# Low parts on GpSimd, a gate in three passes, shorter means, and residual work moved in a two-block transformer kernel

## The reference, cut to what matters

```python
h = x @ w_in + b_in                       # 1024 -> conv_a, conv_g, q, k, v, r, f_lr, gate_a, gate_b
u = a * sigmoid(g)
u = depthwise_conv(u, 31 taps) + conv_b
u = silu(layer_norm(u, ln_g, ln_b))       # mean and variance over the 1024 channels
y_conv = u @ w_co + b_co
y_gla = gla_branch(q, k, v, r, f_lr, ...) @ w_o
merged = sigmoid(gate_a) * y_conv + sigmoid(gate_b) * y_gla
x = layer_norm(alpha * x + merged @ w_out + b_out, ln1_g, ln1_b)
x = layer_norm(alpha * x + hier_moe(x), ln2_g, ln2_b)   # 64 experts, 8 groups, top 2 of one group
# then the second block (four branches, a feed-forward layer)
```

## Time and profile before

| | us |
|---|---|
| median of 3 runs | 1696.02 (1695.73 to 1697.38) |
| the profiled execution, whole | 1695.62 |
| its span in the trace | 1693.5 |
| PE, DVE, ACT, POOL busy in the span | 1361.7, 674.6, 472.0, 58.8 |

### The profile page before, as it was taken

One profiled execution on the slowest core, in us unless ns is written; L12 is line 12 of the kernel. 1 busy time (PEld: TensorE's weight loads), 2 busy tenths in 40 slices (PEclk: granted clock), 3 DMA queues, 4 the chain that ended last, 5 costly groups with the idle time before them and its releaser, 6 DMA issues.

```text
span 1693.5 us, 21308 instructions
## 1 busy us (share of the span) xinstructions
PE 1361.7 (80%) x8592; PEld 883.3 (52%) x8592; DVE 674.6 (40%) x1109; ACT 472.0 (28%) x682; POOL 58.8 (3%) x27
## 2 busy tenths in 40 slices
PE   8999999876666756666676666566799999999998
PEld 7889988522122212221221222122399999778887
DVE  4788979311001101110110011011267888655874
ACT  4464233401001001000010010010264864456653
POOL 0000000670000000000000000000000000000000
PEclk9999999889788879887887888888899999999999
DMA  8433555799999999999999999999944325475440
GB/s 345 152 144 150 213 206 247 307 432 429 431 431 431 433 431 432 432 432 431 430 433 433 432 432 431 432 430 432 421 188 150 131 73 196 174 254 176 180 174 25
DMA packets 50441, 530.79 MB, mean 313 GB/s; under 512 B 4276, under 2 KB 5556, under 8 KB 33862
## 3 DMA queue, kind: packets, MB, share of 16 engines
q1 hardware_dynamic: 50374, 529.86, 75.6%
HBM read 528.80 MB, written 1.05 MB: 313 GB/s over the span
## 4 chain that ended last, share of the span: by engine, by line
PE 53%; DMA 36%; DVE 6%; ACT 3%; issue 1%; DVEq 0%; SPq 0%; ACTq 0%
DMA shared<-in_w 36%; PE psum L1429 6%; PE psum L454 6%; PE psum L456 6%; PE psum L455 6%; PE psum L367 5%; PE psum L1450 4%; PE psum L2216 4%; PE psum L1456 3%; PE psum L1402 3%; PE psum L2217 2%; PE psum L2053 1%; DVE ring_parts L590 1%; PE psum L611 1%; PE psum L2187 1%
## 5 line engine op out<-in xcount | busy, mean ns | idle before, releaser
L1429 PE MATMUL psum<-ring,arena 128*32 128x512 f32 x992 | 142.7, 727 | 85.5 <-DMA ring<-in_w 85.4
L1429 PE MATMUL psum<-shared,arena 128*32 128x512 f32 x1040 | 147.8, 712 | 63.4 <-DMA shared<-in_w 63.3
L1659 DVE TENSOR_TENSOR shared<-shared,psum 128x512 f32<-128x512 f32 x16 | 11.0, 689 | 457.4 <-PE psum L1429 457.4
L1450 PE MATMUL psum<-shared 128*32 128x512 f32 x512 | 90.5, 843 | 67.0 <-DMA shared<-in_w 67.0
L454 PE MATMUL psum<-parts 128*128 128x256 f32 (+1 forms) x424 | 135.8, 320 | 0.7 <-DVE parts L532 0.7
L455 PE MATMUL psum<-parts 128*128 128x256 f32 (+1 forms) x424 | 134.4, 317 | 0.0
L456 PE MATMUL psum<-parts,ring_parts 128*128 128x256 f32 x464 | 131.2, 283 | 0.0
L1429 PEld LDWEIGHTS psum<-ring,arena 128*32 128x32 f32 x992 | 33.8, 130 | 182.2 <-DMA ring<-in_w 99.0
L456 PE MATMUL psum<-parts 128*128 128x256 f32 (+1 forms) x392 | 125.4, 320 | 0.0
L1429 PEld LDWEIGHTS psum<-shared,arena 128*32 128x32 f32 x1040 | 37.4, 127 | 168.3 <-issue 89.8
L454 PE MATMUL psum<-parts,ring_parts 128*128 128x256 f32 x400 | 114.8, 287 | 0.4 <-ACT shared L2250 0.4
(11 more groups left out here) (341 smaller groups left out, 2350.0 us busy)
## 6 DMA issues: line engine op xcount, KB each, us to landing
shared<-in_w SPq DMA_DIRECT2D x47, 4096.0 KB, 32.7
ring<-in_w SPq DMA_DIRECT2D x47, 4096.0 KB, 32.5
ring<-in_w_in SPq DMA_DIRECT2D x19, 2048.0 KB, 8.5
ring<-in_w_ffn_gate_up SPq DMA_DIRECT2D x11, 2048.0 KB, 8.1
ring<-in_w_gate SPq DMA_DIRECT2D x8, 2048.0 KB, 8.1
ring<-in_w_ffn_down SPq DMA_DIRECT2D x5, 2048.0 KB, 7.8
ring<-in_w_out SPq DMA_DIRECT2D x4, 2048.0 KB, 8.3
shared<-in_w SPq DMA_DIRECT2D x6, 1024.0 KB, 28.7
```

The source lines that it names most:

```text
L1429: m = pe.matmul(ps[slots, bank, :], V.picked[:, k, slots], w[e * len(w) // QUAD][:, e % (QUAD // len(w)), j, :], start=(k == 0), stop=(k = ...
L1450: m = pe.matmul(ps[slots, MOE_BANK["down"][c], :], V.hidden_t[:, f, slots], w(e), start=(f == 0), stop=(f == ET - 1))
```

## The change

1. `InSplit` takes in gb0 and gb1 (units 44 to 51), so the second gate's 8 tiles are made in three passes. ACT makes their high parts and evaluates their sigmoids within its loop. `moe_read0` is given behind gb1 and no more behind ga1.
2. The low parts of units 28 to 51 (24 units) are made by POOL (`block1_pool`). DVE's loop keeps its steps for units 28 to 43 but without the low part, and with 6 taps per unit in place of 4 (3 in place of 1 at units 39 and 40).
3. Before the mean DVE adds the 8 tiles to one (1024, 512, 256 columns), and PE makes one product. The centring and the squares go in two halves; DVE adds the squares to one tile, PE makes one product for the variance.
4. The scaling by the reciprocal goes tile by tile, between the parts of the tiles; ACT makes the high parts of the odd tiles. The products `gate_gla` and some low parts change places.
5. Residual rows (alpha, b_out), the constants of the router and the router's column sums (now a product and three additions) go from DVE to POOL. DVE waits for the rows before `gate_conv(4)`, since b_out lies where merged tiles 4 to 7 go.
6. PE's wait for `mem_ms` moves from the beginning of `moe_pe` into the first quad, behind the last products that pick rows.

```diff
-    SLABS = ["g0", "a1", "g1", "k", "v0", "v1", "q", "r0", "r1", "ga0", "ga1"]
-    BUFS = 3
+    SLABS = ["g0", "a1", "g1", "k", "v0", "v1", "q", "r0", "r1", "ga0", "ga1", "gb0", "gb1"]
+    BUFS, POOLED = 3, 28
...
     slab_tiles("ga1", "ga", 4)
+    for s in range(2):
+        slab_tiles(f"gb{s}", "gb", 4 * s)
     pe.drain().then_inc(S("moe_read0"), FREED)
-    for s in range(2):
-        pe_slab_tiles(K, pe, B, R, f"gb{s}", tiles("gb", 4 * s, 4), x)
...
-    pe_group(K, pe, B, "conv_mean", [K.c("j1024")] * DT, [conv[:, j, :] for j in range(DT)])
+    pe_group(K, pe, B, "conv_mean", [K.c("j1024")], [K.A(1, T)])
...
-    pe.wait_ge(S("conv_squares"), 1)
-    pe_group(K, pe, B, "conv_var", [K.c("j1024")] * DT, [squares[:, j, :] for j in range(DT)])
+    pe.wait_ge(S("gla_conv"), GLA_CONV["squares_sum"])
+    pe_group(K, pe, B, "conv_var", [K.c("j1024")], [K.A(1, T)])
...
-    for n in range(split.units):
-        split.low(L, n)
+    for n in range(4 * InSplit.SLABS.index("gb0")):
+        if n < split.POOLED:
+            split.low(L, n)
...
-        pace = 0 if done < 0 else 2 if done < 4 or 8 <= done < 12 else 4
+        pace = 0 if done < 0 else 2 if done < 4 or 8 <= done < 12 else 4 if n < split.POOLED else 6
...
     dve.wait_ge(taps, CW * DT)
+    add(K.A(1, 1024), K.A(3, 1024), K.A(3, 1024, 1024))
+    add(K.A(1, 512), K.A(1, 512), K.A(1, 512, 512))
+    add(K.A(1, T), K.A(1, T), K.A(1, T, T))
     dve.sem_inc(S("gla_conv"), 1)
...
-    L.done(dve.tensor_tensor(conv, conv, wide(K.rstd(0), DT), ALU.mult), S("conv_normed"))
-    gate_gla(6)
-    for m in range(DT):
-        act_parts(m)
+    for m in range(DT):
+        L.done(dve.tensor_tensor(conv[:, m, :], conv[:, m, :], K.rstd(0), ALU.mult), S("conv_normed"))
+        if m:
+            act_parts(m - 1)
+        if m in (2, 4):
+            gate_gla(m // 2 + 1)
+    act_parts(DT - 1)
...
+        if m == 4:
+            dve.wait_ge(S("sums_rows"), ROWS_ADDED)
...
-    B.wait_read(pe, "mem_ms")
     pe.wait_ge(S("chosen"), 1)
...
                         pick(6, DT)
+                        B.wait_read(pe, "mem_ms")
...
+def block1_pool(K, pool):
+    S, W, V, L = K.sem, router_views(K), moe_views(K), K.line("pool", pool)
+    step, x1 = S("pool_steps"), K.tiles(1, TT, D)
+    split = InSplit(K)
+    for n in range(split.POOLED, split.units):
+        split.low(L, n)
+    pool.wait_ge(S("router_in"), 32)
+    def column_sums(name, scaled, out):
+        gain = last(K.v(name, 0, DT), NG + NE)
+        L.done(pool.tensor_tensor(scaled, V.w_router, gain, ALU.mult), step)
+        s = W.partial
+        L.done(pool.tensor_tensor(s[:, 0:4, :], scaled[:, 0:4, :], scaled[:, 4:DT, :], ALU.add), step)
+        L.done(pool.tensor_tensor(s[:, 0:2, :], s[:, 0:2, :], s[:, 2:4, :], ALU.add), step)
+        L.done(pool.tensor_tensor(out, s[:, 0, :], s[:, 1, :], ALU.add), S("sums_rows"))
...
+    pool.wait_ge(S("x_rows_in"), 16)
+    L.done(pool.tensor_scalar(K.A(1), K.A(1), ALPHA1, None, ALU.mult), step)
+    K.wait_gain(pool, "b_out")
+    for t in range(TT):
+        L.done(pool.tensor_tensor(x1[:, t, :], x1[:, t, :], K.gain("b_out"), ALU.add), S("sums_rows"))
```

More of the change, by code:

```diff
@@ L876, in outputs @@
             evac(f"ga{m}", K.tiles(8, DT)[:, m, :], ACT.Sigmoid, bias=K.v("b_ga", m))
+        elif slab in ("gb0", "gb1"):
+            m = i + 4 * int(slab[2])
+            evac(f"gb{m}", K.tiles(9, DT)[:, m, :], ACT.Sigmoid, bias=K.v("b_gb", m))
     kdec, o = K.tiles(10, TT, GDK, TT * GDK), K.tiles(4, DT)
@@ L904, in block1_act @@
                    B, "o_ms")
-    for m in range(DT):
-        evac(f"gb{m}", K.tiles(9, DT)[:, m, :], ACT.Sigmoid, bias=K.v("b_gb", m))
     end = EndSplit(K)
@@ L1114, in merged_low @@
         L.done(dve.tensor_tensor(end.m8[1][:, m, :], m8[:, m, :], end.m8[0][:, m, :].bitcast(F32), ALU.subtract), S("x_low"))
-    def router_sums(name, scaled, out):
-        gain = last(K.v(name, 0, DT), NG + NE)
-        L.done(dve.tensor_tensor(scaled, V.w_router, gain, ALU.mult), S("dve_steps"))
-        L.done(dve.tensor_reduce(out, scaled.rearrange("p k n -> p n k"), AX, ALU.add), S("router_sums"))
-    for m in range(4):
-        gate_gla(m)
-    lows(0, 2)
+    gate_gla(0)
     b = B.wait_full(dve, "conv_mean")
-    L.read(dve.tensor_tensor(conv, conv, wide(ps[:, b, 0:T], DT), ALU.subtract), B, "conv_mean")
+    mean = wide(ps[:, b, 0:T], DT // 2)
@@ L1127, in block1_dve @@
+    L.done(dve.tensor_tensor(conv[:, 0:4, :], conv[:, 0:4, :], mean, ALU.subtract), S("gla_conv"))
+    L.read(dve.tensor_tensor(conv[:, 4:DT, :], conv[:, 4:DT, :], mean, ALU.subtract), B, "conv_mean")
     dve.sem_inc(S("gla_conv"), 1)
+    dve.wait_ge(S("conv_squares"), 1)
+    add(K.A(1, 512), K.A(1, 512), K.A(1, 512, 512))
+    add(K.A(1, T), K.A(1, T), K.A(1, T, T))
+    dve.wait_ge(S("conv_squares"), 2)
+    add(K.A(1, 512, 1024), K.A(1, 512, 1024), K.A(1, 512, 1536))
+    add(K.A(1, T, 1024), K.A(1, T, 1024), K.A(1, T, 1280))
@@ L2990, in _ @@
         def _(pool):
+            block1_pool(K, pool)
             moe_pool(K, pool)
```

76 lines of the change are left out of this document (43 added, 33 removed).

## The result

| | before | after |
|---|---|---|
| median, us | 1696.35 (1695.73 to 1697.38, 4 runs) | 1722.38 (1722.11 to 1722.71, 4 runs) |
| the profiled execution, us | 1695.62 | 1722.14 |
| its span, us | 1693.5 | 1720.4 |

The changed kernel takes 1.0155 times as long, with a 95% interval of 1.014 to 1.017. It is slower, as forecast, but by 26 us where the forecast was 8, and the time lies 1.4 us beyond the range's upper end of 1721.

The account below looks back on a forecast made before the run. PE was half the chain and DMA a third; everything hung on PE's first slab read, with PE and DVE full before the mean. +13.9 - 6.0 + 1.0 + 4.4 - 3.3 - 2.2 = +7.8, rounded +8, on 1695.6 gave 1704 us; range 1678 to 1721 us.

Parts of the forecast that it names:

- its 4.7 us: Second gate: 8 three-pass tiles at 2.88 us, 23.0 us, replace 64 plain products of 27.7 us; PE gains 4.7 us.
- 4 x 0.44 = 1.75 us: Conv taps: a POOL low part of 1024 columns holds DVE 1.75 us, scaled from 0.44 us for 256; likeliest case, chance 0.42.
- The row of 0.73 us at 315.13 us: Profile before: DVE's 128x128 product beside a POOL instruction took 0.73 us against a 0.29 us median, read as held 0.44 us.
- whole duration: Rival: each POOL low part holds DVE for all its 2.37 us, giving 1720 us; chance 0.10.
- 24 x 1.75 = 42 us: Before the mean: 24 POOL low parts hold DVE 42 us; holds hidden by PSUM work and waits for PE about balance.
- a forecast of 240: Before the mean: DVE done at 114.55 + 82.3 + 42 = 239 us, with a POOL column sum 240 us; mean 13.9 us late.
- PE to stall at `o_rstd`: Before the mean: if DVE is held, PE idles about 6 us before `o_rstd` and 10 us before the mean.
- +4.4 us: Behind the variance: POOL's residual rows, with a pass of about 2 us, hold DVE's scaling and parts about 4.4 us.
- -6.0 + 1.0: Mean and variance: single PE products gain 3.0 us each, 6.0 together; the chain behind the variance loses 1 us.
- it is in the range, not in the sum: PE's clock: a 10 us stall before the mean may add 2 to 5 us to every slow case; not summed.
- -3.3: Behind co7: DVE is rid of column sums and residual rows; gain of 3.3 us, bounds 0 and 3.6 us.
- -2.2: Start of the mixture: PE's moved wait for `mem_ms` gains 2.2 us, between `chosen` at 308.64 and PE's start at 310.98 us.

Follow-up runs that it names:

- Plain gate and 5 taps: Changed kernel with second gate in plain float32, low parts, residual rows and column sums on DVE, 5 taps a unit from unit 28: 1688.01 us.
- three passes and 6 taps: Changed kernel with all 52 low parts, residual rows and column sums on DVE, 6 taps a unit from unit 28, three-pass gate kept: 1693.79 us.
- the fills: Changed kernel with POOL writing zeros into the low parts of units 28 to 51 instead of subtracting, so reading nothing: 1690.32 us.
- plain gate, POOL empty: Changed kernel with second gate in plain float32, low parts 0 to 43, residual rows and column sums on DVE, 4 taps a unit: 1691.49 us.
- the profile of 1707.00 us: Changed kernel with residual rows and column sums back on DVE, 24 low parts still on POOL; executions over two runs from 1705.13 to 1729.03 us.
- copies: Changed kernel with POOL copying the source into the low parts of units 28 to 51, one input read instead of two: 1690.96 us.

## Why the prediction was right in kind and short in size

**Bound and direction.** The reading of the chain held: all of the difference had arisen by the first slab read, and none behind it. That POOL's reads hold DVE, that DVE's taps are the bound before the mean, and that the change is therefore slower, is what the runs show.

**The gate.** Its tiles came at 2.88 us, as forecast, and PE gained its 4.7 us; with DVE full it can't use them. Plain gate and 5 taps beats three passes and 6 taps by 5.8 us, both without POOL; three passes put 8 low parts, 9.7 us, on DVE.

**What POOL does to DVE: the step "4 x 0.44 = 1.75 us".** This is the step that failed ahead of the mean. The hold of a low part is 2.15 us, not 1.75. The row of 0.73 us at 315.13 us stood beside an instruction that took 41 us for 256 columns, a power (`ALU.pow`), so reading can't be what filled its time, and the scaling by columns from it was not sound. The row nearest in kind was POOL's plain product with two inputs, 0.73 us for 256 columns. At its whole duration it prices a low part at 2.37 us, which is close. That was the rival "whole duration", to which I gave 0.10. The Trainium skill (SBUF — State Buffer, Who interferes with whom) calls the shared pair of ports an exclusive lock, and states the block for the whole instruction where it speaks of DVE's 2-port modes. The low parts beside two-input taps bear that out to 2.15 us of 2.4. It also says that a GpSimd instruction that only writes doesn't contend with DVE's second input, and the fills agree: 0 us. A low part that begins beside a tap takes up to 2.70 us where others take 2.38; whether that is where the remaining 0.25 us are, no run separates.

**The sum before the mean.** I had 24 x 1.75 = 42 us, and had put the waits for PE against the holds that waits and PSUM work hide, as even. Of the 24 low parts, 19 met DVE's SBUF work (5, 4, 5 and 5 in four stretches of taps and `gate_head`, 10.7 + 8.1 + 10.8 + 10.8 = 40.4 us). Five fell into waits and PSUM work, 10.8 us at the same price, and against them stand 8.2 us in which DVE waited for PE between the states and 1.7 us of gaps. So that balance held in number, though 4.9 of the 8.2 us are the clock's (below). At 2.15 us the 24 cost 9.6 us more than forecast, and the column sums, for which I had 1 us, have 3.6 us (74 taps in 43.81 us, of which 29.4 are their own and 10.8 the five low parts'). These two terms make the error of 10 us, less 1.2 us because the stretch began that much sooner than I had it. By the rows: 113.35 us (start) + 127.2 us (busy, 44.0 of them hold; 42.6 by the comparison above, where the taps stand in shorter runs) + 8.2 (waits for PE) + 1.7 (gaps) = 250.5 us, against a forecast of 240. I had expected PE to stall at `o_rstd`; it stood for 6.6 us at the first state instead.

**Rows on POOL: the step "+4.4 us".** The pass over 128x2048 was put at about 2 us. Beside DVE's scaling it took 5.37 us, and it held DVE's instruction with one input too. The hold was 8.5 us, and the piece cost 10.7 us in all. This was the second largest error, 6.3 us. DVE itself had only 2.48 us to spend there.

**Means.** "-6.0 + 1.0" for the products and the chain came to 44.0 - 46.7 = -2.7 us (plain gate, POOL empty), and -2.4 with 5 taps. There PE is at the first parts 6.05 us sooner after the mean's start, as forecast, and takes 3.7 us longer from there to co7. Some 2.1 us of these are the clock at 0.50 from 245 to 251 us, by the distance of the products. That leaves 1.6 us for the chain, near the 1.0 I had. So most of what was missing is the clock, and it falls there without any long wait. In the kernel before, where PE comes to the parts 6 us later, it stays at 1.00.

**Clock: the step "it is in the range, not in the sum".** It was put at nothing in the sum, and rows show it in three places. Ahead of the mean it is the 4.9 us between the first two states, and they come through. From the start of the taps ahead of the first state (113.35 us in the changed kernel) to the first `gate_head` it takes 55.35 us in the changed kernel, 51.07 us in the profile of 1707.00 us, and 43.70 us both with fills and with copies. The holds ahead of the first state are 10.7, 6.5, 0 (fills) and 2.4 us (copies). So PE has room for some 4 us of delay and takes up the copies' 2.4 us whole. Beyond that it waits (6.6 and 2.4 us), loses 4.9 us of clock, and DVE waits for it in turn. Behind the mean it is the 2.1 us above. Long waits ahead of the mean (8.8, 9.6 and 20.9 us) lengthen the piece to co7 further, from 44.0 to 44.9 us to 46.8, 47.0 and 45.7 us, so by 0.8 to 3.0 us; beside the rows it is at most the 2.4 us that the hold leaves over.

**Behind co7 and `mem_ms`.** -3.3 was -2.5 to -2.8. -2.2 was -2.8 in the profile after, and alone -2.6 in the profile and -2.6 to -2.9 in the time. Both hold. That last piece is 21.0 us in most versions and 22.0 to 22.3 in four, the changed one among them. In these four PE's 24 products that pick rows take 5.46 us, in six of the others 4.46 to 4.54 us; in the one pair whose windows were read, the granted clock is 0.50 for longer in the first.

**The range.** The upper end was the whole-duration case, 1720 us, with no clock and no more than 1.5 us of extra hold from the rows. It should have been that case plus the clock's 2 to 5 us. Of the 19 us by which the sum was short, 10 lie before the mean and 9 between it and co7.

## What to carry to other kernels

Moving work with two SBUF inputs from DVE to POOL can pay only where DVE works on PSUM or waits: here DVE spends 1.22 us on such an instruction itself and loses 2.15 us when POOL makes it beside two-input SBUF work. Look first whether DVE is merely waiting with work in hand: one more independent piece between two waits (5 taps for 4) gave 3.5 us for nothing. When you add holds along DVE's queue, follow them through to PE's waits and back: here a delay under 4 us was taken up, and one over it came back with 4.9 us of clock. And look at PE's clock also where you only take products from it.

## What the runs showed of the hardware that was not expected

- POOL's read of two inputs of 1024 columns (2.34 to 2.46 us alone) holds DVE's work on two SBUF inputs for 2.15 us, a copy of one input (1.04 us at its shortest, 1.46 us in the mean) for 0.9 us, a fill (0.955 us) not at all. DVE's `norm_heads`, with one input in PSUM, was not held beside a low part (2.46 us for two).
- It goes the other way too. In the changed kernel the longest low part took 6.4 us (2.4 alone), beside a run of taps that had begun ahead of it:

```profile
L533 POOL TENSOR_TENSOR parts<-ring,parts x24: 2342/2456/6422, 113.4 to 215.7; 128x1024 fp32r<-128x1024 f32 x24
```

- It began at 164.63 us and ended when 18 undisturbed taps (7.21 us from 161.56 us) and its own time were over. In other stretches a low part gets in after one tap. What decides between the two was not found. The two lower levels of the program that spread from 1705 to 1729 us differ in it; whether the upper one does was not seen.
- POOL's multiplication of 128x2048 elements by a constant took 5.36 to 5.41 us in the five traces that have it, 2.6 ns per column, more than the 2.2 ns of its product of two inputs, and it held even DVE's conversion with one input (1.56 us in place of 0.29). In all of them it stood beside DVE's scaling, and one on 256 columns (L1718 in the kernel before, at 357.16 us) takes 0.40 us, so how much of the 5.4 us is its own is not shown.
- PE was at 1.2 GHz behind waits of 6.6 and 5.9 us, until about 142 and 286 us, and with plain gate and 5 taps also from 245 to 251 us, ahead of which it had been busy for 3.41 of 5 us and had no wait over 1.1 us.
